# A three-layer transformer kernel: four feature tiles at a time by token in the last layer's projections, later norm steps there, and a buffer of its own for the group norm's roots

## The reference

```python
# blocks 1 and 2
h = rms_norm(x, attn_norm_w[layer]); u = h @ w_in[layer]
o_main = retention(...) or diff_attention(...)      # q, k, v, g are columns of u
x = x + concat([o_main, o_mem]) @ w_out[layer]
x = x + (silu(gate) * up) @ w_down[layer]           # gate, up = rms_norm(x) @ w_gate_up
# block 3
proj = rms_norm(x) @ w_in                           # z, xbc, dt, q, k, v, f
y_ssd = ssd_mixer(xbc, z, dt, ...)                  # ends in a norm over groups of 512 features
qh, kh = rms_norm(heads(q)), rms_norm(heads(k))     # 16 heads of 64
logits = qh @ kh.T * scale + cum[q] - cum[k]        # causal
y_fox = softmax(logits) @ heads(v)
x = x + concat([y_ssd, y_fox]) @ w_out
x = x + (silu(gate) * val) @ w_down                 # a conv over tokens of rms_norm(x) @ w_up
```

## Time and profile before

| | |
|---|---|
| median of 3 runs | 1041.55 us |
| the profiled execution's own time | 1041.01 us |
| its span | 1039.2 us |
| PE busy | 1025.1 us, 99% |
| DVE busy | 796.5 us, 77% |
| ACT busy | 635.4 us, 61% |
| POOL busy | 236.8 us, 23% |
| granted TensorE clock, mean | 0.998 |

### The profile page before, as it was taken

The page is one execution under the profiler, slowest core; times in us unless marked ns, Lnnn a source line. Parts: engine busy times, 40 slices in busy tenths (PEclk is TensorE's granted clock), DMA queues, the critical chain, the costliest instruction groups (busy, mean ns, idle before and its releaser), DMA issues.

```text
span 1039.2 us, 21815 instructions
## 1 busy us (share of the span) xinstructions
PE 1025.1 (99%) x7372; PEld 942.4 (91%) x7372; DVE 796.5 (77%) x1301; ACT 635.4 (61%) x1188; POOL 236.8 (23%) x204
## 2 busy tenths in 40 slices
PE   8999999999999999999999999999999999999998
PEld 7989988888889898888888899999898999999988
DVE  6875897877665988988777569978968579999853
ACT  7754775665554667766666456766666666666532
POOL 3200044444110000244443110000201034444300
PEclk9999999999999999999999999999999999999999
DMA  8543465655665332655666654543333355555563
GB/s 299 184 140 94 129 224 192 186 191 179 199 187 184 122 103 71 212 189 184 194 186 186 200 186 155 166 159 123 112 132 122 131 165 193 182 182 182 179 204 104
DMA packets 52483, 174.36 MB, mean 168 GB/s; under 512 B 5952, under 2 KB 7232, under 8 KB 52288
## 3 DMA queue, kind: packets, MB, share of 16 engines
q1 hardware_dynamic: 52416, 173.46, 52.1%
HBM read 172.39 MB, written 1.05 MB: 167 GB/s over the span
## 4 chain that ended last, share of the span: by engine, by line
PE 55%; DVE 5%; ACT 2%; issue 1%; DMA 0%; DVEq 0%; SPq 0%; ACTq 0%
PE bank L773 7%; PE bank L771 6%; PE bank L772 6%; PE scores L773 4%; PE scores L769 4%; PE scores L767 4%; PE bank L767 3%; PE bank L769 3%; PE scores L772 2%; PE scores L771 2%; PE scores L766 2%; PE bank L766 2%; PE bank L799 2%; PE bank L800 2%; PE bank L801 2%; DVE ring_parts L1735 1%
## 5 line engine op out<-in xcount | busy, mean ns | idle before, releaser
L1735 DVE TENSOR_TENSOR ring_parts<-ring_raw,ring_parts 128x1024 fp32r<-128x1024 f32 (+2 forms) x343 | 421.4, 1232 | 34.6 <-ACT ring_parts L1225 28.9
L1225 ACT ACTIVATE ring_parts<-ring_raw 128x1024 fp32r<-128x1024 f32 (+2 forms) x343 | 341.5, 999 | 63.2 <-PE scores L767 28.1
L773 PE MATMUL bank<-xw_parts,ring_parts 128*128 128x256 f32 x648 | 182.2, 281 | 0.0
L771 PE MATMUL bank<-xw_parts,ring_parts 128*128 128x256 f32 x472 | 136.6, 289 | 0.3 <-DVE con L1880 0.2
L772 PE MATMUL bank<-xw_parts,ring_parts 128*128 128x256 f32 x472 | 133.4, 283 | 0.0
L773 PEld LDWEIGHTS bank<-xw_parts,ring_parts 128*128 128x128 f32 x648 | 123.4, 190 | 7.5
L799 PE MATMUL bank<-ring_parts,xw_parts 128*128 128x256 f32 x384 | 112.9, 294 | 0.2 <-DVE u L1923 0.2
L800 PE MATMUL bank<-ring_parts,xw_parts 128*128 128x256 f32 x384 | 108.5, 283 | 0.0
L801 PE MATMUL bank<-ring_parts,xw_parts 128*128 128x256 f32 x384 | 108.4, 282 | 0.0
L773 PE MATMUL bank<-act_parts,ring_parts 128*128 128x256 f32 x381 | 107.8, 283 | 0.0
L1655 POOL TENSOR_TENSOR act_parts<-tmp,act_parts 128x256 f32 (+1 forms) x66 | 61.7, 935 | 166.3 <-ACT act_parts L1301 166.3
(11 more groups left out here) (273 smaller groups left out, 2555.0 us busy)
## 6 DMA issues: line engine op xcount, KB each, us to landing
ring_raw<-w_up SPq DMA_DIRECT2D x132, 512.0 KB, 3.6
ring_raw<-w_in SPq DMA_DIRECT2D x85, 512.0 KB, 3.6
ring_raw<-w_down SPq DMA_DIRECT2D x48, 512.0 KB, 3.5
ring_raw<-w_down SPq DMA_DIRECT2D x24, 384.0 KB, 4.0
ring_raw<-w_oa SPq DMA_DIRECT2D x16, 256.0 KB, 2.6
ring_raw<-w_ob SPq DMA_DIRECT2D x16, 256.0 KB, 2.9
ring_raw<-w_oa SPq DMA_DIRECT2D x8, 512.0 KB, 3.6
ring_raw<-w_ob SPq DMA_DIRECT2D x8, 512.0 KB, 3.6
```

The lines of the kernel that those rows point to most:

```text
L771: mm(ps[:, 0:T], w_hi, high(parts, t), start=start, stop=False)
L773: return mm(ps[:, 0:T], w_lo, high(parts, t), start=False, stop=stop)
L1225: A(ring_hi[:, slot * DM:slot * DM + width], ring_raw[:, slot * DM:slot * DM + width], ACT.Copy).then_inc(hi_done, 1)
L1735: V.tensor_tensor(ring_lo[:, a:b], ring_raw[:, a:b], ring_hi[:, a:b].bitcast(f32), SUB).then_inc(lo_done, 1)
```

## The change

1. In the first layer the values' first two pairs (tiles 6 to 9), and in the last layer all queries, keys and values, are computed four tiles at a time over four slots (`project_four`): two input tiles a slot, 512 weight columns moving, one PSUM bank for each half of the tokens. The two banks of the projection are filled together. A semaphore `first_tokens` says that the first half of the tokens is complete, in the middle of the fourth slot; `evac_four` copies out the first bank then and the second at `tile_done`. A slot has 12 matmuls of 512 columns in place of 24 of 256.
2. `ORDER` is changed: two query tiles with the two key tiles of the same heads, and values after each two such fours in the last layer; two tiles are swapped forward in the first.
3. In `plans()` the last layer's norms have other slots (queries and keys of a four are there at the same time), and fox_values waits for the values' four.
4. Squares wait only for the last use of the same buffer, the heads have four places, and the group norm's roots have a buffer of their own.

```diff
+FOURS = {"in0": (6,), "in1": (), "in2": (20, 22, 24, 26, 36, 40)}
@@ project
+                if ph.of_four(c) is not None:
+                    project_four(ph, c, parts, slot, halfway)
+                    return
+            def project_four(ph, c, parts, slot, halfway):
+
+                part = ph.of_four(c)
+                for tt in range(2):
+                    n = ph.out(0, c - part) + tt
+                    if part == 0:
+                        pe.wait_ge(out_ready, ph.freed_out(n))
+                    if halfway and tt:
+                        halfway(c)
+                    for k in range(2):
+                        t = ph.inputs[2 * part + k]
+                        a = slot * DM + k * 2 * T
+                        o = bank[ph.bank_of[n]][:, :]
+                        w_hi, w_lo = ring_hi[:, a:a + 2 * T], ring_lo[:, a:a + 2 * T]
+                        x_hi, x_lo = (m(parts, t)[:, tt * P:(tt + 1) * P] for m in (high, low))
+                        mm(o, x_hi, w_hi, start=part == 0 and k == 0, stop=False)
+                        mm(o, x_hi, w_lo, start=False, stop=False)
+                        last = mm(o, x_lo, w_hi, start=False, stop=part == 3 and k == 1)
+                    if part == 3 and tt == 0:
+                        last.then_inc(first_tokens, 1)
+                last.then_inc(tile_done, 1)
@@ VectorE, in a slot after the EARLY steps
+                    if ph.of_four(c) == 3:
+                        evac_four(ph, c)
+            def evac_four(ph, c):
+
+                fours_done[0] += 1
...
+                for tt, (done, count_) in enumerate(((first_tokens, fours_done[0]), (tile_done, ph.tile(0, c)[1] + 1))):
+                    dve.wait_ge(done, count_)
...
+                    V.tensor_scalar(dst, src, rstd_tok[:, tt:tt + 1], None, MUL).then_inc(out_ready, 1)
@@ plans
-    for j in range(4):
-        a = 21 + 6 * j
-        norm(2, a + 2, 20 + 2 * j)
-        norm(2, a + 4, 28 + 2 * j)
...
+    for j, end in enumerate((24, 28, 36, 40)):
+        for slot, t in ((end, 20 + 2 * j), (end + 1, 28 + 2 * j)):
+            norm(2, slot, t)
+            if j:
+                for at_, kind in ((slot, "squares"), (slot + 1, "norm")):
+                    plan[2][at_].remove((kind, t))
+                    plan[2][at_].insert(0, (kind, t))
...
-            at(2, slot + 3, "fox_values", p)
+            at(2, max(slot + 3, 33 if j < 2 else 45), "fox_values", p)
@@ squares, group norm
-                if n >= 2:
-                    act.wait_ge(np_out, n - 1)
+                last_use = last_norm_in(n)
+                if last_use:
+                    if heads_by_token(*last_use[1:]):
+                        act.wait_ge(head_ms, number["head_stat", last_use] + 1)
...
-                roots(n, normed(n)[:, 0:T], 1.0, 0, norm_bank(n)[:, 0:T])
+                roots(n, group_roots[:, :], 1.0, 0, norm_bank(n)[:, 0:T])
```

More of the change, by code:

```diff
@@ L149, in by_token, with of_four @@
     def by_token(self, c):
-        return c in self.wide or c - 1 in self.wide
+        return c in self.wide or c - 1 in self.wide or self.of_four(c) is not None
+    def of_four(self, c):
+        return next((c - a for a in self.fours if a <= c < a + 4), None)
     def halves(self, i, c):
@@ L158, in finishes @@
     def finishes(self, c):
-        return c % self.per == self.per - 1 and c not in self.wide
+        return c % self.per == self.per - 1 and c not in self.wide and self.of_four(c) is None
     def bank(self, i, c):
@@ L195, in at, with after_like @@
         plan[layer][slot].append((kind, *key))
+    def after_like(layer, slot, step):
+        steps = plan[layer][slot]
+        n = next((i for i, other in enumerate(steps) if other[0] != step[0]), len(steps))
+        steps.insert(n, step)
     def norm(layer, slot, tile, soon=False):
@@ L203, in norm @@
         at(layer, slot + 1, "norm", tile)
-        plan[layer][slot + 2].insert(0, ("spread_soon" if soon else "spread", tile))
+        after_like(layer, slot + 2, ("spread_soon" if soon else "spread", tile))
         if soon:
@@ L207, in norm @@
         else:
-            plan[layer][slot + 3].insert(0, ("norm_out", tile))
+            after_like(layer, slot + 3, ("norm_out", tile))
     def unit(layer, slot, kind, h, maps=1):
@@ L319, in plans @@
     at(2, 18, "ssd_steps", 1)
[L320 to L327 removed]
+    for j, end in enumerate((24, 28, 36, 40)):
[5 more added lines that the diff above has]
+                    plan[2][at_].insert(0, (kind, t))
         for n in range(2):
[L329 removed]
+            p, slot = 2 * j + n, 28 + 6 * j + 3 * n
             at(2, slot, "fox_scores", p)
@@ L479, in program @@
         stored = sem("stored")
+        first_tokens = sem("first_tokens")
         block = ctx.enter_context(nc.Block())
@@ L585, in program, with last_norm_in @@
                         count("fill", (layer, filled(layer, key[0], key[1])[0]))
+        def last_norm_in(n):
+            had = [(m, k) for (kind, k), m in number.items()
+                   if kind == "norm" and k[0] == "norm" and m < n and m % 2 == n % 2]
+            return max(had)[1] if had else None
         def turn_bank(layer, t):
@@ L635, in arrived @@
                 last = order.index(t)
+                four = PH[f"in{layer}"].of_four(last)
+                last += 0 if four is None else 3 - four
                 eng.wait_ge(out_ready, PH[f"in{layer}"].out(0, last) + 1)
@@ L1768, in step @@
                             split_lo(ph, j, d)
+                    if ph.wide and i == 0 and c == 3:
+                        root_by_token(q)
                     if ph.finishes(c):
```

52 lines of the change are left out of this document (37 added, 15 removed).

## The result

The changed kernel takes 1046.60 us (median of 5 runs, 1045.58 to 1048.51), the kernel before 1041.34 (5 runs, 1040.71 to 1041.59): 1.0056 times as long, 95% interval [1.0045, 1.0067]. That is 5.3 us slower, outside the predicted range. The profiled execution of the changed kernel took 1048.43 us with a span of 1046.6, so it lies near the top of its runs (the record has a mean granted clock of 0.997 for it and for the run of 1048.51, and of 0.998 for the three of 1045.58 to 1046.60); against the profiled execution before (span 1039.2) the difference to be found is 7.4 us.

The account below looks back on a forecast made before the run. PE, busy 99% of the span, was taken as the bound: its stream plus few waits. Terms -2.25 + 0 + 0 + 1.9 = -0.35 us gave 1040.7 for the profiled execution, 1041.2 as median; whole range 1038.2 to 1043.9.

Parts of the forecast that it names:

- Term 4: Waits in the last layer: 5.2 us of new PE waits, old 3.3 gone; net +1.9 us, bounds -3.3 and +4.5.
- (b): Start of slot 33: PE waits 1.4 us for the first bank, copied out by DVE after the reciprocal.
- (d): Start of slot 45: the output projection's first tile waits 2.0 us for DVE to empty the first bank.
- (a): End of slot 30: PE's ssd_decay 13 waits 0.8 us for ACT's exponential of decay 12, behind squares and roots.
- (c): End of slot 42: PE waits 1.0 us, with ACT's squares and roots in front of fox_probs 4.
- Term 1: Width: 336 wide matmuls replace 672 narrow ones, each saving 0.0067 us; -2.25 us, bounds 0 and 3.9 us saved.
- Term 3: First layer's four: DVE has room to copy the first bank in time, so 0 us.
- Term 2: Copies and ring: slightly longer DVE copy-outs, loads unchanged, no PE wait behind them; 0 us, bounds 0 and 0.6.
- B: Rival, chance 0.13: DVE reaches copy-outs late at slots 25, 33 and 45; 1 us later gives 1043.8 us.
- A: Rival, chance 0.31: the fours' waits do not come or only replace old ones; 1039.3 or 1037.7 us.
- C: Rival, chance 0.06: the width saves less; 1042.6 us by the skill's rule, 1043.4 with no saving.
- My marks: Predicted profile signs: 7036 matmuls, wide ones 0.233 us apart, waits at (a) to (d), output projection's first matmul at 793.0.

Follow-up runs that it names:

- x7: Changed kernel with 8 unused 512-column matmuls on PE ahead of slot 33's wait and 11 ahead of slot 45's, order unchanged: 1044.23 us, ratio 1.0034 to the kernel before.
- x1: Changed kernel with VectorE copying both banks out before fox_probs' reciprocal in a four's last slot: 1041.90 us, ratio 1.0004 to the kernel before.
- x2: Changed kernel with the next tiles' squares and roots behind fox_probs and ssd_decay on ScalarE in slots 29 and 41: 1046.78 us, ratio 1.0054 to the kernel before.
- x3: Changed kernel with the edits of x1 and x2 together: 1042.17 us, ratio 1.0010 to the kernel before.
- x9: x5 with each 512-column matmul of a four issued as two of 256: 1041.25 us, ratio 1.0000 to the kernel before.
- x4: Changed kernel with each 512-column matmul of the fours issued as two of 256, all else the same: 1047.61 us, ratio 1.0049 to the kernel before.
- x5: Changed kernel copying the first bank when full, then ssd_skip and norm_out, the second bank, fox_probs: 1040.19 us, ratio 0.9992 to the kernel before.
- x11: The kernel of x5 run once more, in a later comparison: 1040.48 us, ratio 0.9991 to the kernel before.

## Why the prediction was wrong

**Term 4, the failed step.** The mechanism was right at all four places, the price was not. I priced a wait as the time in which PE stands still ("Wait: 1.4", "Wait: 2.0") and took the stream behind it to run at full pace. Behind (b) and (d) it ran at half, which adds 3.2 us that no term held. x7 takes this away without touching the order and gains 2.4 us in the median and 3.5 in the stage; x1 shortens both waits and loses both falls. In the last layer the trace before does not show a fall, as its longest wait there was 1.5 us and the clock stayed at 1.00 behind it. But its mean clock of 0.998 stood in the table, and the stretch from 10 to 13 us shows half the clock behind a wait of 1.49 us. I read neither, and never bounded a wait's cost from above by what a slower clock behind it would add.

**Term 4, the waits' size.** (a) 1.1 for 0.8, (b) 1.9 for 1.4, (c) 1.1 for 1.0, (d) 2.6 for 2.0: 6.7 in place of 5.2. The rest, 1.2 us, are short waits at slots where I had none (0.3 for the decay, 0.9 for turns of normed tiles). That the old waits for fox probabilities and ssd_weights (3.1 of the 3.3) go was right. Net +4.6 for +1.9, just past the +4.5 of my bound. At (b) the maxima are 2.9 us later than in my walk: PE came 1.4 us later into this layer (slot 21 at 689.80 for 688.35), the ring's product of 1.21 us took 1.78 just ahead of them, and the gate's product L2239 took 0.95 (735.25) where it had taken 0.42 (L2162 before, 731.38). Both lie under GpSimd's subtractions (734.81 to 738.91). I had taken the norm's steps out from under these, rightly (0.69 and 0.17 us now), and had put nothing in their place. No run takes GpSimd away, so that it is the cause is not shown. The remaining 0.3 us I can't place by a row of its own.

**Term 1, the width.** -2.25 was too little. The mean distance of wide matmuls of the fours is 0.230 us (225 in the changed kernel), of narrow ones 0.1195 (528 before): 0.0091 each, 3.1 us for 336. The reading from the short rows (0.2333) was the worse one; the bound of 3.9 held. The first stage's 0.46 us for 48 says about the same (0.0096). The Trainium skill's rule of 2.5 ns an instruction ("TensorE: Matmul & The Clock Gate", Back-to-back issue gap), an estimate of 0.84 us, falls short of this by almost four times.

**Term 3, the first layer.** 0 was wrong in both halves: 0.4 us gained in its stage and some 0.8 lost at 428 us. This part is suggested by two pairs of medians and thirteen profiles, and its mechanism is open.

**Term 2** held: no wait of PE between 690 and 810 us is put down to the ring, and 7036 matmuls are there.

By these terms -3.1 + 4.6 + 3.2 + 0.8 = 5.5, against 7.4 in the profiled pair, from which the waits and both falls are read. The last layer's two projections should be 4.6 + 3.2 - 2.6 = 5.2 longer (2.6 for the 288 wide ones there) and are 6.0, and the second layer has 1.9 where the term has 0.8: so 1.9 us are not assigned. That 5.5 lies near the 5.3 of the medians is luck. The median run has a mean clock of 0.998, and x2's profile with one fall has 0.998 too, where two falls give 0.997; with one fall the terms give 3.9.

**The rivals.** B, at 0.13, was the nearest in place and time. Its mechanism, DVE later than in my walk because GpSimd's subtractions meet other DVE steps, is there, but it accounts only for the 1.1 us by which (b) and (d) are over it, and nothing waits at slot 25. A was wrong: the waits came. C was wrong: a wide matmul saves more than I had taken, not less. My marks were half met: the two entries behind the copy-out are there, one over 2.5 us; the output projection's first matmul starts at 798.69, past the 794.5 at which I called the forecast wrong. The high end of 1043.9 rested on waits alone. x10 shows what the change could be: with the first bank copied early and no four in the first layer it is 1.5 us faster than before, 0.14%. Its interval lies below 1, though by less than the 0.2% I had named as the smallest difference to be told.

## What to carry to other kernels

Filling two banks together turns a copy-out into something that PE waits for in the middle of a slot, so put the copy ahead of every step on the same engine that waits for a third engine. Price a new PE wait not only by its length: look at the granted clock behind it, and look at every stretch of the trace below full clock, at the start too; where a new wait is as long as one that a fall followed, add as an upper bound what one fall cost (1.6 us each here). A wait removed from one customer of a shared engine is often handed to the next (x2, x3), and a faster PE finds new waits (x9): a saving per matmul reaches the time only in part.

## What the runs showed of the hardware

- TensorE's granted clock fell to half behind waits of 1.93 and 2.60 us, in a kernel that kept PE 98% busy, and stayed there for some 3 us of full work (744.4 to 748, 799 to 802.5). In the same place it fell at both waits of x4 (1.9 and 2.5) and behind 2.04 in x2, and did not behind 1.91 in x2, so five of six. Behind waits of 1.3 (x1), 1.5 (the last layer before) and 0.7 us (x5) it stayed at 1.00. In the first 14 us, where PE works little, it fell behind less: behind 1.49 us in the kernel before, and in x11 behind 0.87 us with 0.65 shortly ahead of it (0.71 from 8 to 10 us, 0.50 from 10 to 11). So the length of one wait alone does not decide it.
- The page "TensorE: Matmul & The Clock Gate" of the Trainium skill says of the clock, in its section What's actually happening, that "the default state is throttled, and activity releases the throttle". The trace agrees in so far as activity holds the clock up: in x7 the same hold filled with matmuls keeps 1.00.
- When the fall comes is not fixed by the wait's end. At slot 33 of the changed kernel the slow matmuls begin 0.8 us after PE had started again (744.43), at slot 45 0.4 us after (799.13). In x4 it came in the wait itself: from 796 to 798 us PE is busy for 0.00 us and the clock is 0.91, and PE starts at 798.01.
- Executions of one kernel differ by it: in x4 1044.7 to 1045.0 us at a mean clock of 1.00 and 1047.6 to 1048.0 at 0.997; in the changed kernel 1045.6 to 1046.6 at 0.998 and 1048.4 to 1048.5 at 0.997.
- DVE's product for the ring (L1792 and its like, 128x1024) and a subtraction of GpSimd start within 0.05 us of each other ahead of the maxima of fox pairs 1 and 5. In the eleven kernels with the last layer changed, 15 times of 22 the product took 1.76 to 1.80 us and GpSimd's step 0.7, and 7 times the product took 1.21 and GpSimd's step 1.8. So one of the two is short and the other long, and one kernel's two places can differ (x1: 1.21 and 1.80). That moves the maxima behind it by 0.6 us.
